# A two-layer encoder trunk on one core: first layer's memory keys projected ahead of the head pairs, one mask matmul a head, last group in two sums

## The chip, the cores and the metric

The kernel runs on one core of a Trainium2 chip. It is one program with five instruction streams: TensorE (PE), VectorE (DVE), ScalarE (ACT), GpSimd (POOL) and the queue of SyncE (SP), which loads the weights. The metric is the device time of one execution in microseconds (us).

## What is computed

Two layers work on x, 256 tokens by 2048 features in float32, with 256 memory tokens beside it. Each layer has a token mixer (layer 0: latent attention with 16 heads and a mask by chunks of 64 tokens; layer 1: stick-breaking attention with 16 heads, strictly causal), then 4 heads of attention into the memory, then a feed-forward network with a causal convolution of width 3. A root-mean-square norm stands before each.

```python
for i in range(DEPTH):                       # DEPTH = 2
    h = _rmsnorm(x, norm_mix[i])
    x = x + (_mla(h, cos, sin, ...) if i % 2 == 0 else _stick_breaking(h, ...))
    x = x + _mem_cross_attn(_rmsnorm(x, norm_mem_q[i]), _rmsnorm(mem, norm_mem_kv[i]),
                            mem_w_q[i], mem_w_kv[i], mem_w_o[i])
    x = x + _conv_ffn(_rmsnorm(x, norm_ffn[i]), ffn_w_in[i], ffn_conv_w[i], ffn_conv_b[i], ffn_w_out[i])
return _rmsnorm(x, norm_final)
```

In `_mla`, `down = h @ w_down` gives a query latent (512 wide, "cq"), a key/value latent ("ckv") and one rotary key ("krope"); each latent has a norm of its own. The keys of the memory are `hm @ w_kv[:, :512]` with `hm` the normed memory: they depend on nothing of x.

## The kernel before

**Weights.** All weights lie in HBM as one stream of 802 units of 128x1024 numbers (512 KB) in the order in which PE uses them (`stream_plan`). SP loads unit v into slot v mod 4 of `w_raw`. ACT copies it, rounded, to `w_hi` (`split`, L469), DVE writes the rest `w_raw - w_hi` to `w_lo` (L846). Both do this three units ahead of PE, in the same in-order queues as all their other work. Operands are split alike: ACT writes the high half (`operand_hi`, L487), DVE the low half (`operand_lo`, L868).

**Matmuls.** `unit` multiplies one weight unit. A chunk of 128 output features with one k takes high weights times [high|low] operand in one matmul 512 wide (L1309), plus low weights times high operand 256 wide (L1316): "two parts", whose sums lie in the two halves of a bank and are added later by `take_low` (ACT) and `take_sum` (DVE). With `parts=1` the first is done as two matmuls 256 wide (L1311, L1312) into the same half, and no adding is needed. Which phases use which is in `in_one_part`. A unit of two k has 4 chunks.

**Order in layer 0.** PE does cq (8 units), ckv (8), krope (2), then 8 stages of two heads each (`mla_stage`: rotary queries r, queries q, keys k, values v, one unit each, with the previous pair's attention between them), then memk0 (8 units, the memory keys, with the last pair's attention between them: `mla_tail`), then the output projection wo0 in four groups g, the memory attention and the feed-forward. Norm statistics: POOL squares and adds the tiles of a norm's input (`sum_squares`, L406, L408), PE averages the result over the partitions (`stat`, or `first_stat` for the first one, L1701, in ckv after its third unit), ACT takes the root and DVE refines it (`find_rstd`, L880 to L886). Then DVE scales the sums of a bank by it (`times_rstd`, L862).

**Memory.** POOL loads the memory in lots of four tiles into a ring of two lots (`load_mem`, L413). In `early_memory` ACT and DVE turn the first 8 tiles into operands during the stages of pairs 0 and 1, and the other 8 during memk0.

**Attention.** `mla_scores` gives one head's scores in bank 4: content and rotary products for the first 128 queries, a mask matmul in bf16 (64 columns, L1380), the same for the other 128, and a second mask matmul (L1383). DVE finds the row maxima (`row_tops`, L919), ACT takes the exponentials, DVE divides (`normalise`, L930), PE transposes (L1391) and multiplies by the values (L1400). `stick_logits` has two mask matmuls of 128 columns (L1492, L1494) in the same way.

**End.** The last group of the last feed-forward, out1_3 (22 units), is done in one part; then DVE adds its four tiles to x, the final norm follows, and the output is stored.

## Time and profile before

| | |
|---|---|
| median of 3 runs | 2391.85 us (2391.81 to 2393.09) |
| the profiled execution: time, span | 2391.88 us, 2389.7 us |
| mean granted clock of TensorE | 0.996 of full |
| PE, DVE, ACT, POOL busy | 99%, 70%, 52%, 13% of the span |
| weight loads | 802 of 512 KB, 3.3 us to landing; HBM 180 GB/s over the span |

The span runs from the first to the last instruction of the profiled execution. A matmul's end is modelled, so "busy" on PE covers a matmul's passage through the array and not only its columns; how fast PE goes is read from the starts of its matmuls.

### The profile page before, as it was taken

The numbers are of one execution on the slowest core, as the hardware profiler recorded it, in microseconds if no ns is written. First come the engines' busy times: TensorE is split into PE (matmuls) and PEld (weight loads), VectorE is DVE, ScalarE is ACT, GpSimd is POOL, SyncE is SP. The second block draws the span as 40 slices with busy tenths as digits, with TensorE's granted clock in tenths as the row PEclk, the third lists the DMA queues.
The fourth block names the chain that finished last, engine by engine and source line by source line (L and its number), as shares of the span: only waits on it lengthen the run. The fifth ranks groups of instructions, "written<-read, shape, count | busy, mean of one in ns | idle before, by whom it ended". The sixth has DMA issues, their size and how long they took to land.

```text
span 2389.7 us, 41908 instructions
## 1 busy us (share of the span) xinstructions
PE 2357.6 (99%) x14608; PEld 2107.5 (88%) x14608; DVE 1679.2 (70%) x2474; ACT 1234.0 (52%) x1860; POOL 300.7 (13%) x305
## 2 busy tenths in 40 slices
PE   9899999999999999999999999999999999999997
PEld 8799898888888888889899998889888888888897
DVE  8876678777877875555755556778778778775544
ACT  5445455655555654444555445455556556564442
POOL 7500225000000000111320000315000000001110
PEclk9999999999999999999999999999999999999999
DMA  7444554555555656555554445545555555556553
GB/s 260 145 137 162 187 176 156 193 189 184 192 187 183 194 191 204 190 189 185 177 177 164 163 164 170 191 160 174 188 184 192 189 180 195 192 180 197 187 187 122
DMA packets 122071, 432.42 MB, mean 181 GB/s; under 512 B 13424, under 2 KB 17776, under 8 KB 121968
## 3 DMA queue, kind: packets, MB, share of 16 engines
q1 hardware_dynamic: 118992, 423.94, 53.3%
q0 software_dynamic: 1440, 5.24, 0.7%
q10 hardware_dynamic: 1536, 1.80, 0.2%
q8 instruction: 72, 1.18, 0.2%
q14 instruction: 31, 0.25, 0.0%
HBM read 428.83 MB, written 2.10 MB: 180 GB/s over the span
## 4 chain that ended last, share of the span: by engine, by line
PE 93%; DVE 6%; ACT 1%; issue 0%; DMA 0%; DVEq 0%; SPq 0%; ACTq 0%
PE bank L1309 49%; PE bank L1316 28%; PE bank L1311 3%; PE bank L1312 3%; DVE w_lo L846 2%; PE bank L1331 2%; PE bank L1333 2%; PE bank L1332 2%; DVE h L868 1%; PE bank L1400 1%; ACT w_hi L469 0%; PE bank L1401 0%; PE bank L1391 0%; PE bank L1381 0%; DVE x L903 0%; PE bank L1491 0%
## 5 line engine op out<-in xcount | busy, mean ns | idle before, releaser
L846 DVE TENSOR_TENSOR w_lo<-w_raw,w_hi 128x1024 fp32r<-128x1024 f32 x802 | 1004.5, 1255 | 533.1 <-ACT w_hi L469 531.7
L469 ACT ACTIVATE w_hi<-w_raw 128x1024 fp32r<-128x1024 f32 x802 | 845.6, 1058 | 751.1 <-PE bank L1316 675.4
L1309 PE MATMUL bank<-h,w_hi 128*128 128x512 f32 x3392 | 1047.5, 396 | 3.2 <-DVE h L868 1.9
L1316 PEld LDWEIGHTS bank<-h,w_lo 128*128 128x128 f32 x3664 | 661.5, 188 | 138.8
L1316 PE MATMUL bank<-h,w_lo 128*128 128x256 f32 x3664 | 701.0, 279 | 0.0
L1309 PEld LDWEIGHTS bank<-h,w_hi 128*128 128x128 f32 x3392 | 525.9, 189 | 16.0 <-DVE h L868 2.1
L1309 PE MATMUL bank<-act,w_hi 128*128 128x512 f32 x1632 | 513.2, 396 | 0.0
L1316 PEld LDWEIGHTS bank<-act,w_lo 128*128 128x128 f32 x2272 | 403.9, 189 | 72.5
L1316 PE MATMUL bank<-act,w_lo 128*128 128x256 f32 x2272 | 443.5, 280 | 0.0
L1309 PEld LDWEIGHTS bank<-act,w_hi 128*128 128x128 f32 x1632 | 248.4, 189 | 0.1
L1311 PE MATMUL bank<-act,w_hi 128*128 128x256 f32 x640 | 168.9, 288 | 0.4 <-DVE attn L862 0.4
L1312 PE MATMUL bank<-act,w_hi 128*128 128x256 f32 x640 | 166.6, 284 | 0.0
L406 POOL TENSOR_TENSOR sq<-x 128x256 f32<-128x256 f32 x101 | 117.6, 1165 | 359.5 <-DVE x L903 354.6
L773 ACT ACTIVATE act<-tmp 128x256 f32 (+1 forms) x88 | 36.8, 418 | 180.7 <-DVE tmp L1224 180.7
L404 POOL TENSOR_TENSOR acc<-x 128x256 f32<-128x256 f32 x7 | 4.3, 614 | 994.1 <-DVE x L903 990.4
L763 ACT ACTIVATE tmp<-tmp,cols 128x256 f32<-128x256 f32 x176 | 104.5, 594 | 46.2 <-DVE tmp L862 46.1
L1311 PEld LDWEIGHTS bank<-act,w_hi 128*128 128x128 f32 x640 | 123.7, 193 | 2.3 <-issue 0.6
L1312 PEld LDWEIGHTS bank<-act,w_hi 128*128 128x128 f32 x640 | 123.7, 193 | 0.1
L408 POOL TENSOR_TENSOR acc<-acc,sq 128x256 f32<-128x256 f32 x126 | 118.6, 941 | 9.9
L851 DVE TENSOR_TENSOR tot<-low,bank 128x256 f32<-128x256 f32 x272 | 112.3, 413 | 0.1
L1215 DVE SCALAR_TENSOR_TENSOR tmp<-tmp,cols 128x256 f32<-128x256 f32 x176 | 85.3, 485 | 23.9 <-DVE tmp L1212 1.6
L476 ACT ACTIVATE low<-bank 128x256 f32<-128x256 f32 x272 | 97.9, 365 | 0.0
(153 smaller groups left out, 1943.7 us busy)
## 6 DMA issues: line engine op xcount, KB each, us to landing
w_raw<-stream SPq DMA_DIRECT2D x802, 512.0 KB, 3.3
tmp<-mem_in POOLq DMA_DIRECT2D x10, 512.0 KB, 4.8
out<-attn SPq DMA_DIRECT2D x5, 256.0 KB, 2.7
x<-x_in SPq DMA_DIRECT2D x4, 256.0 KB, 5.3
x<-x_in SPq DMA_DIRECT2D x2, 512.0 KB, 8.5
out<-attn ACTq DMA_DIRECT2D x3, 256.0 KB, 2.2
cols<-cols_in ACTq DMA_DIRECT2D x1, 420.5 KB, 5.1
mats<-mats_in ACTq DMA_DIRECT2D x1, 320.0 KB, 5.8
```

The source lines that it names most:

```text
L406: step(nc.gpsimd.tensor_tensor(sq[:, :], tile, tile, ALU.mult))
L408: step(nc.gpsimd.tensor_tensor(acc[:, :], acc[:, :], sq[:, :], ALU.add))
L469: nc.scalar.activation(w_hi[:, s, :], w_raw[:, s, :], ACT.Copy).then_inc(hi_split, 1)
L476: nc.scalar.activation(low[:, t % 2, :], banks[bank][:, TOK:2 * TOK], ACT.Copy).then_inc(low_copied, 1)
L763: nc.scalar.activation(conv[:, j % 2, :], u_ext[:, j % 2, 2:TOK + 2], ACT.Identity, scale=conv_col(2, 4 * g + j + is_up * FT, it), bias=co ...
L846: nc.vector.tensor_tensor(w_lo[:, s, :], w_raw[:, s, :], w_hi[:, s, :], ALU.subtract).then_inc(lo_split, 1)
L851: nc.vector.tensor_tensor(tot[:, t % 2, :], low[:, t % 2, :], banks[bank][:, 0:TOK], ALU.add).then_inc(tile_summed, 1)
L1215: nc.vector.scalar_tensor_tensor(conv[:, j % 2, :], u_ext[:, j % 2, 0:TOK], conv_col(0, c, it), conv[:, j % 2, :], ALU.mult, ALU.add).then ...
L1309: mm(bank[:, :], w_hi[:, s, c:c + P], a, start=first and i == 0, stop=False)
L1311: mm(bank[:, 0:TOK], w_hi[:, s, c:c + P], a[:, 0:TOK], start=first and i == 0, stop=False)
L1312: mm(bank[:, 0:TOK], w_hi[:, s, c:c + P], a[:, TOK:2 * TOK], start=False, stop=False)
L1316: ins = mm(bank[:, 0:TOK], w_lo[:, s, c:c + P], a[:, 0:TOK], start=False, stop=last and i == len(ks) - 1)
```

## The change

**Memory keys first.** memk0 moves in the weight stream and on every engine from behind the head pairs to between ckv and krope. Its 16 operand tiles are made by ACT and DVE during the last two units of cq, in ckv and in the first two units of memk0 (`KEYS_AT`), with semaphores of their own (`key_hi`, `key_lo`); POOL issues two loads of the memory after six tiles of its first sum of squares, the third after the thirteenth, behind a wait for four key tiles, and the fourth after the sixteenth. The memory is loaded again for its norm and again for the values' operands: 14 loads in all, where there were 10. The sums of memk0 are added unscaled into `mem_k` during krope and scaled in wo0_0. The steps that stood in krope (low halves of the ckv latent, table angles, roots) move to memk0. `early_memory` goes.

**Last heads beside wo0_0.** The last pair's attention (`mla_tail`) stands between the units of wo0_0, and so do the norm of the memory, the four scalings of `mem_k` and the operands of memory tiles 8 to 15 for the values. For this the banks of the groups are exchanged (`half`), in layer 1 too (`stick_banks`, `STICK_Z`).

**One mask matmul a head.** The mask operand is stored twice side by side, and one bf16 matmul (2x64 columns; stick-breaking 2x128) writes both places at the end of the scores.

**Last group in two sums.** out1_3 does its first 19 units in two parts into one set of banks, the last 3 in one part into another. ACT and DVE add the first sum to x beside the last 3 units.

```diff
-        (phase[:3] != "out" or phase[-2:] == "_3")
+        (phase[:3] != "out" or phase == "out0_3")
...
+def two_sums(phase):
+    return phase == "out1_3"
...
@@ -79,6 +88,7 @@
         if layer == 0:
             phase("cq", 8, 4, 4)
             phase("ckv", 8, 4, 4)
+            phase("memk0", 8, 4, 4)
             phase("krope", 2, 1, 1)
...
-        phase(f"memk{layer}", 8, 4, 4)
+        if layer:
+            phase(f"memk{layer}", 8, 4, 4)
...
+FIRST_SUM = {0: (0, 1), 1: (2,), 2: (3,)}
...
-            return 0 if g % 2 else 4
-        EARLY_MEMORY = {(0, 2): (0,), (0, 3): (1, 2), (1, 0): (3,), (1, 1): (4,), (1, 2): (5,), (1, 3): (6, 7)}
...
+            return 4 if g % 2 else 0
+        KEYS_AT = {("cq", 6): (0, 1), ("cq", 7): (2, 3), ("ckv", 0): (4, 5), ("ckv", 1): (6, 7), ("ckv", 3): (8,), ("ckv", 4): (9,),
+                   ("ckv", 5): (10,), ("ckv", 6): (11, 12), ("ckv", 7): (13,), ("memk0", 0): (14,), ("memk0", 1): (15,)}
...
             if layer == 0:
-                return (h[:, k, :], act[:, 8 + k, :], True) if first else (act[:, 8 + k, :], act[:, 8 + k, :], False)
-            return (act[:, HEADS + k, :], act[:, HEADS + k, :], False) if first else (h[:, k, :], act[:, k, :], True)
+                return act[:, k, :], act[:, 8 + k, :]
...
             for n in range(KT):
+                if n == 6:
+                    load_mem(0)
+                    load_mem(1)
+                if n == 13:
+                    pool.wait_ge(key_lo, 4)
+                    load_mem(2)
                 pool.wait_ge(x_landed[x_lot(n)], 16)
                 sum_squares("mix0", n, KT, x[:, n, :])
-            load_mem(0)
-            load_mem(1)
+            pool.wait_ge(key_lo, 8)
+            load_mem(3)
             for name in ("cq", "ckv"):
...
+            pool.wait_ge(key_lo, KT)
+            load_mem(0)
+            load_mem(1)
...
-                if l == 5:
+                first_keys("ckv", l)
+            for l in range(8):
+                split(PLAN["memk0"][0] + l + AHEAD)
+                if l < LT:
+                    times_rstd(latent[:, LT + l, :], whole("ckv", 7, l, 4 + l), rstd_x).then_inc(latent_ready, 1)
+                first_keys("memk0", l)
+                n = l - 1
+                if 0 <= n < LT:
+                    k = HEADS + LT + n
+                    operand_lo(act[:, k, TOK:2 * TOK], latent[:, LT + n, :], GAIN["ckv"] + n, act[:, k, 0:TOK], OP0["ckv"] + n)
+                if l == 2:
                     rope_angle()
-                if l == 7:
+                if l == 4:
                     rope_cos()
+                if l == 6:
+                    find_rstd("cq", rstd_q, 5, D_MODEL / LORA)
...
-                for n in (2 * l, 2 * l + 1):
-                    times_rstd(latent[:, LT + n, :], whole("ckv", 7, n, 4 + n), rstd_x).then_inc(latent_ready, 1)
-                for n in (2 * l, 2 * l + 1):
-                    k = HEADS + LT + n
-                    operand_lo(act[:, k, TOK:2 * TOK], latent[:, LT + n, :], GAIN["ckv"] + n, act[:, k, 0:TOK], OP0["ckv"] + n)
-                if l == 0:
-                    find_rstd("cq", rstd_q, 1, D_MODEL / LORA)
+                for j in (2 * l, 2 * l + 1):
+                    take_sum(PLAN["memk0"][2] + j, j, to=mem_k[:, j, :])
+            find_rstd("ckv", rstd_kv, 6, D_MODEL / LORA)
...
+                        if g == 0 and l in ahead_of:
+                            ahead_of[l]()
                         split(PLAN[f"wo{layer}_{g}"][0] + l + AHEAD)
                         if g == 0 and l == 0:
-                            find_rstd(f"memkv{layer}", rstd_m[:, :], half(0) + 3)
+                            find_rstd(f"memkv{layer}", rstd_m[:, :], MEMORY_STAT[layer])
                         if g == 0 and l < 4:
-                            times_rstd(mem_k[:, l, :], take_sum(PLAN[f"memk{layer}"][2] + l, l), rstd_m).then_inc(scaled, 1)
+                            keys = take_sum(PLAN[f"memk{layer}"][2] + l, half(1) + l) if layer else mem_k[:, l, :]
+                            times_rstd(mem_k[:, l, :], keys, rstd_m).then_inc(scaled, 1)
+                        if g == 0 and l in tail:
+                            tail[l]()
+                        if layer == 0 and g == 0 and l < 4:
+                            mem_lo(layer, 8 + 2 * l, True)
+                            mem_lo(layer, 9 + 2 * l, True)
...
+                        side(l)
+                        if two_sums(phase):
+                            for j in FIRST_SUM.get(l - (n - LAST_WHOLE), ()):
+                                first_sum = take_sum(t0 + j, half(g + 1) + j)
+                                nc.vector.tensor_tensor(x[:, 4 * g + j, :], x[:, 4 * g + j, :], first_sum, ALU.add).then_inc(first_added, 1)
             def no_side(l):
...
                 mm(b[:, 0:P], q_sb[:, e, i, 0:P], k_sb[:, e, i, 0:P], start=True, stop=False)
-                mm(b[:, 0:P], qr_sb[:, e, 0:P], kr_sb[:, i, 0:P], start=False, stop=False)
-                mm(b[:, CHUNK:P], MASK_ROWS, MASK_COLS, start=False, stop=True)
-                mm(b[:, P:3 * P], q_sb[:, e, i, P:2 * P], k_sb[:, e, i, :], start=True, stop=False)
-                mm(b[:, P:3 * P], qr_sb[:, e, P:2 * P], kr_sb[:, i, :], start=False, stop=False)
-                mm(b[:, 2 * P + CHUNK:3 * P], MASK_ROWS, MASK_COLS, start=False, stop=True).then_inc(s_done, 1)
+                mm(b[:, 0:P], qr_sb[:, e, 0:P], kr_sb[:, i, 0:P], start=False, stop=True)
+                mm(b[:, P:3 * P], q_sb[:, e, i, P:2 * P], k_sb[:, e, i, :], start=False, stop=True, skip_group_check=True)
+                mm(b[:, P:3 * P], qr_sb[:, e, P:2 * P], kr_sb[:, i, :], start=False, stop=True, skip_group_check=True)
+                late_keys = b.rearrange("p (t n) -> p t n", t=2)[:, :, CHUNK:P]
+                mm(late_keys, MASK_ROWS, MASK_COLS, start=False, stop=True, skip_group_check=True).then_inc(s_done, 1)
...
-                mm(z[:, 0:P], IDENT_BF, NEG_STRICT, start=False, stop=True, skip_group_check=True)
                 mm(z[:, TOK:TOK + P], k_sb[:, e, i, P:2 * P], q_sb[:, e, i, P:2 * P], start=False, stop=True, skip_group_check=True)
-                mm(z[:, TOK:TOK + P], IDENT_BF, NEG_STRICT, start=False, stop=True, skip_group_check=True).then_inc(z_done, 1)
+                diagonal = z.rearrange("p (t n) -> p t n", t=2)[:, :, 0:P]
+                mm(diagonal, IDENT_BF, NEG_STRICT, start=False, stop=True, skip_group_check=True).then_inc(z_done, 1)
...
+            def first_memory():
+                for l in range(8):
+                    pe.wait_ge(key_lo, 2 * l + 2)
+                    unit(PLAN["memk0"][0] + l, (2 * l, 2 * l + 1), 4 * P, lambda j: j, lambda k: kept_memory(0, k)[0], l == 0, l == 7,
+                         lambda j: pe.wait_ge(latent_ready, j + 1))
+                    if l == 5:
+                        pe.wait_ge(latent_ready, LT + 2)
+                        stat("cq", 5)
+                pe.wait_ge(latent_ready, LT + 3)
+                stat("ckv", 6)
...
+                        if g == layer:
+                            taken(j)
+                        elif g == 1 - layer:
                             if j == 0:
...
-                    group(f"wo{layer}_{g}", HEADS, half(g), from_act, free, heads_ready if g == 0 else None)
+                    def attend_last(l):
+                        if l in tail:
+                            tail[l]()
+                    group(f"wo{layer}_{g}", HEADS, half(g), from_act, free, heads_ready if g == 0 else None, attend_last if g == 0 else None)
...
-                          parts=1 if in_one_part(f"out{layer}_{g}") else 2)
+                    if two_sums(phase):
+                        v0, n = PLAN[phase][0], FT // 2
+                        m = n - LAST_WHOLE
+                        for l in range(m):
+                            unit(v0 + l, (2 * l, 2 * l + 1), 4 * P, lambda j: half(g + 1) + j, from_act, l == 0, l == m - 1, free_of(phase))
+                        for l in range(m, n):
+                            unit(v0 + l, (2 * l, 2 * l + 1), 4 * P, lambda j: half(g) + j, from_act, l == m, l == n - 1,
+                                 lambda j: summed(PLAN[f"out{layer}_{g - 1}"][2] + j), parts=1)
+                    else:
...
-            stat("cq", 1)
             for l in range(2):
-                unit(v0 + l, tuple(range(8 * l, 8 * l + 8)), P, lambda j: 2, from_h, l == 0, l == 1,
-                     lambda j: pe.wait_ge(latent_ready, 3), parts=1)
+                unit(v0 + l, tuple(range(8 * l, 8 * l + 8)), P, lambda j: 4, from_h, l == 0, l == 1,
...
-            summed(PLAN["out1_2"][2] + 3)
-            stat("final", half(3) + 3, [last_squares(n) for n in range(KT - 4, KT)])
+            pe.wait_ge(first_added, 4)
```

ACT's queue changes as DVE's does: it makes each high half just ahead of the low half shown here. `krope` goes to bank 4, `r0` to bank 7.

Three places, as the instruction streams have them. First POOL, from the thirteenth tile of the first sum of squares to its end and the loads behind it. Before:

```order
L406 TENSOR_TENSOR sq<-x 128x256
L408 TENSOR_TENSOR acc<-acc,sq 128x256
L406 TENSOR_TENSOR sq<-x 128x256
L408 TENSOR_TENSOR acc<-acc,sq 128x256
L406 TENSOR_TENSOR sq<-x 128x256
L408 TENSOR_TENSOR acc<-acc,sq 128x256
L406 TENSOR_TENSOR sq<-x 128x256
L408 TENSOR_TENSOR acc<-acc,sq 128x256
L406 TENSOR_TENSOR sq<-x 128x256
L410 TENSOR_TENSOR acc<-acc,sq 128x256
L413 DMA tmp<-mem_in 128x4x256 x2
```

Now:

```order
L437 TENSOR_TENSOR sq<-x 128x256
L439 TENSOR_TENSOR acc<-acc,sq 128x256
L444 DMA tmp<-mem_in 128x4x256
L437 TENSOR_TENSOR sq<-x 128x256
L439 TENSOR_TENSOR acc<-acc,sq 128x256
L437 TENSOR_TENSOR sq<-x 128x256
L439 TENSOR_TENSOR acc<-acc,sq 128x256
L437 TENSOR_TENSOR sq<-x 128x256
L441 TENSOR_TENSOR acc<-acc,sq 128x256
L444 DMA tmp<-mem_in 128x4x256
L435 TENSOR_TENSOR acc<-attn_49 128x256
```

The load that stands between the thirteenth and the fourteenth tile waits until DVE has made four key tiles; it and the two loads after the sixth tile were behind the sum.

Then PE, from the last chunk of ckv (bank7) on. Before:

```order
L1312 MATMUL bank7<-h,w_hi 128x256
L1316 MATMUL bank7<-h,w_lo 128x256 x2
L1346 MATMUL bank1<-acc,mats 128x256
L1311 MATMUL bank2<-h,w_hi 128x256
L1312 MATMUL bank2<-h,w_hi 128x256
```

Now:

```order
L1394 MATMUL bank7<-h,w_hi 128x256
L1398 MATMUL bank7<-h,w_lo 128x256 x2
L1391 MATMUL bank0<-act,w_hi 128x512 x2
L1398 MATMUL bank0<-act,w_lo 128x256 x2
L1391 MATMUL bank1<-act,w_hi 128x512 x2
L1398 MATMUL bank1<-act,w_lo 128x256 x2
L1391 MATMUL bank2<-act,w_hi 128x512 x2
```

The statistic of cq (bank1) and krope (bank2) followed ckv at once; now the 8 units of memk0 follow, with that statistic after the sixth.

Last DVE, at the start of the unit stretch that holds the last pair's attention: memk0 before, wo0_0 now (small: row maxima and their reciprocals; act<-tmp: operands of the memory). Before:

```order
L846 TENSOR_TENSOR w_lo<-w_raw,w_hi 128x1024
L868 SCALAR_TENSOR_TENSOR act<-tmp,cols,act 128x256 x2
L846 TENSOR_TENSOR w_lo<-w_raw,w_hi 128x1024
L919 TENSOR_REDUCE small<-bank4 128x1 x2
L922 TENSOR_SCALAR small<-small 128x2
L868 SCALAR_TENSOR_TENSOR act<-tmp,cols,act 128x256 x2
L927 RECIPROCAL small<-small 128x2
L930 TENSOR_SCALAR attn_49<-attn_49,small 128x128
L930 TENSOR_SCALAR attn_49<-attn_49,small 128x256
```

Now:

```order
L902 TENSOR_TENSOR w_lo<-w_raw,w_hi 128x1024
L942 TENSOR_SCALAR attn_49<-bank7 128x258
L944 SCALAR_TENSOR_TENSOR attn_49<-rstd_m 128x258
L946 TENSOR_TENSOR attn_49<-attn_49 128x258
L948 SCALAR_TENSOR_TENSOR rstd_m<-attn_49,rstd_m 128x258
L919 TENSOR_TENSOR attn_49<-attn_49,rstd_m 128x256
L925 SCALAR_TENSOR_TENSOR act<-tmp,cols,act 128x256 x2
L902 TENSOR_TENSOR w_lo<-w_raw,w_hi 128x1024
L919 TENSOR_TENSOR attn_49<-attn_49,rstd_m 128x256
L984 TENSOR_REDUCE small<-bank4 128x1 x2
L987 TENSOR_SCALAR small<-small 128x2
L925 SCALAR_TENSOR_TENSOR act<-tmp,cols,act 128x256 x2
L992 RECIPROCAL small<-small 128x2
L995 TENSOR_SCALAR attn_49<-attn_49,small 128x128
L995 TENSOR_SCALAR attn_49<-attn_49,small 128x256
```

Ahead of the division of head 14's probabilities (the last row or two) there now stand five more instructions of the norm's root and scaling (L942 to L919) and one more scaling.

## Rows read from the trace of the kernel before

**Rows 1.** the page, part 1: engine, busy time, share of the span, instructions
```profile
PE 2357.6 (99%) x14608; PEld 2107.5 (88%) x14608; DVE 1679.2 (70%) x2474; ACT 1234.0 (52%) x1860; POOL 300.7 (13%) x305
```

**Rows 2.** waits of PE, 56 to 120 us: total us, times, longest
```profile
PE bank L1411 <- DVE attn L862: 4.4, 2, 3.6
PE bank L1391 <- DVE attn L930: 2.4, 3, 1.4
PE bank L1331 <- DVE attn L862: 1.6, 1, 1.6
PE bank L1346 <- POOL acc L410: 1.1, 1, 1.1
PE bank L1311 <- DVE attn L862: 0.4, 1, 0.4
```

**Rows 3.** PE alone in four stretches: length, busy (count), granted clock, DMA share, GB/s
```profile
72.60:79.30 6.70, 5.65 (x24) 0.50 0.49 157
82.90:86.10 3.20, 2.77 (x13) 0.50 0.54 164
2280.00:2300.00 20.00, 20.00 (x116) 1.00 0.55 187
2340.00:2360.00 20.00, 20.00 (x169) 1.00 0.48 160
```

**Rows 4.** PE by time at the layer change: start, length, what
```profile
1145.98 0.50 PE L1309 MATMUL bank<-h,w_hi 128*128 128x512 f32 x1 [1.88 <-DVE h L868]
```

**Rows 5.** POOL by time: its squares of the input tiles, then two loads
```profile
18.11 1.48 POOL L406 TENSOR_TENSOR sq<-x 128x256 f32<-128x256 f32 x1
...
31.10 1.48 POOL L406 TENSOR_TENSOR sq<-x 128x256 f32<-128x256 f32 x1
...
38.27 1.60 POOL L410 TENSOR_TENSOR acc<-acc,sq 128x256 f32<-128x256 f32 x1
39.81 1.67 POOL L413 DMA_DIRECT2D tmp<-mem_in  x2
```

**Rows 6.** PE by time: the first sum over squares
```profile
42.10 0.38 PE L1701 MATMUL bank<-acc,mats 128*128 128x256 f32 x1
```

**Rows 7.** DVE by time: operands and splits, beside POOL and without it
```profile
28.72 1.71 DVE L868 SCALAR_TENSOR_TENSOR h<-x,cols,h 128x256 fp32r<-128x256 f32 x2
30.36 6.54 DVE L846 TENSOR_TENSOR w_lo<-w_raw,w_hi 128x1024 fp32r<-128x1024 f32 x4
...
52.58 0.70 DVE L960 CAST attn<-attn 128x256 f32<-128x256 int32 x1
...
56.17 0.29 DVE L967 TENSOR_SCALAR attn<-attn 128x256 f32<-128x256 f32 x1
...
207.05 0.88 DVE L868 SCALAR_TENSOR_TENSOR act<-tmp,cols,act 128x256 fp32r<-128x256 f32 x2 [1.38 <-ACT act L487]
```

**Rows 8.** DVE by time: last pair's probabilities, later a norm
```profile
203.71 1.23 DVE L846 TENSOR_TENSOR w_lo<-w_raw,w_hi 128x1024 fp32r<-128x1024 f32 x1 [0.48 <-ACT w_hi L469]
...
208.04 0.55 DVE L930 TENSOR_SCALAR attn<-attn,small 128x128 f32<-128x128 f32 x2
...
229.41 0.42 DVE L880 TENSOR_SCALAR attn<-bank 128x258 f32<-128x258 f32 x1
...
231.70 0.43 DVE L886 SCALAR_TENSOR_TENSOR rstd_m<-attn,rstd_m 128x258 f32<-128x258 f32 x1
```

**Rows 9.** PE by time: transposes of head 14
```profile
209.47 0.38 PE L1391 MATMUL bank<-mats,attn 128*128 128x128 f32 x2
```

**Rows 10.** PE by time: a head's scores and its first mask
```profile
202.80 0.19 PE L1380 MATMUL bank<-masks 128*128 128x64 bf16 x1
202.83 0.68 PE L1381 MATMUL bank<-attn 128*128 128x256 f32 x2
203.34 0.59 PE L1382 MATMUL bank<-attn 128*128 128x256 f32 x2
```

**Rows 11.** the page, part 6: loads of the memory, KB, us to landing
```profile
tmp<-mem_in POOLq DMA_DIRECT2D x10, 512.0 KB, 4.8
```

More of the change, by code:

```diff
@@ L710, in projections @@
                 v0 = PLAN[f"memq{layer}"][0]
-                again = [k for k in range(KT) if kept_memory(layer, k)[2]]
+                again = AGAIN[layer]
                 side = residual_side(f"wo{layer}_3", norm, 3, half(3), EARLY)
@@ L805, in ffn @@
                 for g in range(1, 4):
-                    stage(f"out{layer}_{g}", FT // 2, residual_side(f"out{layer}_{g - 1}", last_norm, g - 1, half(g), EARLY))
+                    phase, side = f"out{layer}_{g}", residual_side(f"out{layer}_{g - 1}", last_norm, g - 1, half(g), EARLY)
+                    n, (v0, _, t0) = FT // 2, PLAN[phase]
+                    for l in range(n):
+                        split(v0 + l + AHEAD)
+                        side(l)
+                        if two_sums(phase):
+                            for j in FIRST_SUM.get(l - (n - LAST_WHOLE), ()):
+                                take_low(t0 + j, half(g + 1) + j, chunk_of(phase, n - LAST_WHOLE - 1, j))
             def no_side(l):
@@ L1156, in projections @@
                 side = residual_side(f"wo{layer}_3", norm, 3, half(3), EARLY)
-                again = [k for k in range(KT) if kept_memory(layer, k)[2]]
+                again = AGAIN[layer]
                 for l in range(8):
@@ L1257, in ffn @@
                 for g in range(1, 4):
-                    stage(f"out{layer}_{g}", FT // 2, residual_side(f"out{layer}_{g - 1}", last_norm, g - 1, half(g), EARLY))
+                    phase, side = f"out{layer}_{g}", residual_side(f"out{layer}_{g - 1}", last_norm, g - 1, half(g), EARLY)
+                    n, (v0, _, t0) = FT // 2, PLAN[phase]
+                    for l in range(n):
+                        split(v0 + l + AHEAD)
+                        side(l)
+                        if two_sums(phase):
+                            for j in FIRST_SUM.get(l - (n - LAST_WHOLE), ()):
+                                first_sum = take_sum(t0 + j, half(g + 1) + j)
+                                nc.vector.tensor_tensor(x[:, 4 * g + j, :], x[:, 4 * g + j, :], first_sum, ALU.add).then_inc(first_added, 1)
             def no_side(l):
```

226 lines of the change are left out of this document (127 added, 99 removed).

## Prediction

> **What bounds the kernel now.** I read the page first. PE is busy 99% of the span [rows 1], so only two things can pay: time that PE loses, and matmuls that take less. The page's slices show the granted clock nowhere below nine tenths, but a slice is 60 us long; so next I read who PE waited for, and the granted clock, in short stretches. The waits are in one place: between 56 and 120 us PE waits nine times, 9.9 us in all [rows 2]. The longest, 3.6 us at L1411, is the rotation of the shared key behind DVE's work on the latents; the others are DVE's too, but for one (POOL, 1.1). In the same place the clock stood at half, 0.50, in two stretches of 6.70 and 3.20 us, with PE busy 5.65 and 2.77 us of them [rows 3]: that is the lower of TensorE's levels, 1.2 GHz, and the reader should note what preceded it, the wait of 3.6 us. At the layer change PE idles 1.88 us [rows 4] and no half clock follows. Elsewhere PE runs without a wait, and there its own rate decides: in 20 us it starts 116 matmuls of a two-part phase (four to a chunk) or 169 of a one-part phase (six to a chunk) [rows 3], so a chunk takes 4 x 20/116 = 0.690 or 6 x 20/169 = 0.710 us, and a unit of four chunks 2.76 or 2.84 us. A few records may be missing, so the difference is good to some 0.007.
>
> **The sum.** It goes from the profiled execution, 2391.88 us (span 2389.7 and 2.2 around it), which is the median of the runs, 2391.85, to 0.03. About 0.2%, 4.8 us, is what a measurement of this kernel can tell from no change.
>
> *Memory keys first.* The 8 units are moved and cost PE the same. What they can give back is what PE loses at 56 to 120 us: 9.9 us of waits; half of 5.65 + 2.77 us of busy time at half clock, 4.2; and, an estimate, 0.15 for each of nine waits, 1.4, since a matmul is shown for 0.38 us [rows 6] though starts come 0.118 apart, so that a wait is counted late. Together 15.5 us. The eight units are 22 us of PE work that waits for nothing of the latents, put in front of everything that does; so the waits of 3.6, 1.1 and 0.4 us go, and the half clock with them. The wait before the first values (L1331, 1.6) has a chain of its own, rotation, a split, scaling, and only the norm of ckv (2.7 us) leaves it: I keep half, 0.8. Of the remaining 3.2 (the second at L1411, three at L1391), pairs 1 and 2, I keep 1.2: the early memory operands, 0.44 us each, go from DVE, but POOL's squares of the memory stay beside it.
>
> Something new is late: POOL. Its first sum of squares ended at 39.87 and PE took it at 42.10 without a wait [rows 5, 6], 2.2 us of room. Now two loads after the sixth tile take 1.67 us [rows 5], so the thirteenth tile is done at 32.8 instead of 31.1, and there POOL waits for the fourth key tile. DVE's queue gives that: from 30.36 the splits of units 8 and 9, two keys, the split of unit 10, two keys. A split is 1.63 us beside POOL (6.54 for four) and 1.23 without, an operand 0.86 or 0.44 [rows 7, 8], successive ones overlap by 0.07, and POOL is idle from 32.8: about 36.1. Then a load, 0.8, and three tiles. Six tiles took 12.99 us from 18.11 to 31.10, 2.17 each, beside one split and two operands a unit, which is the mixture that DVE has again: 43.4. PE waits 1.3 us (bounds: 0, and 3.6 at the 2.9 us a tile of the last three, 31.10 to 39.87). Nothing waits for the later loads: keys 8 to 11 are wanted ten us after theirs. So 1.3 + 0.15 + 0.8 + 1.2 = 3.5 us stay: **-12.0** (bounds -15.5 and -5).
>
> Here the Trainium skill's page "SBUF — State Buffer" (Who interferes with whom) has a rule against the change: a DVE instruction with two SBUF inputs and a GpSimd instruction that reads SBUF lock each other out for a whole instruction. By that rule the trace agrees (1.63 against 1.23, 0.86 against 0.44); what more of it would do is the second rival.
>
> *Last heads beside wo0_0.* The attention is as it was; new ahead of `normalise` of head 14 on DVE are the memory norm's root, 229.41 to 232.13, 2.7 us [rows 8], and two scalings of 0.4. Before, DVE had a wait of 0.48 there [rows 8], the division ended at 208.59 and PE transposed at 209.47 [rows 8, 9], 0.88 later. The statistic's matmuls, now ahead of wo0_0, give about 0.8 more (two passes of 0.38 [rows 6] as an estimate). So 2.7 + 0.8 - 0.5 - 0.9 - 0.8: **+1.3** (bounds 0 and 3.5). Queued behind it are splits, three units ahead of PE: covered. Head 15 has no norm ahead of it.
>
> *Masks.* The first mask starts at 202.80, 0.03 before the next matmul, whose two passes are shown for 0.68 us, where the two of the next one, just as wide, are shown for 0.59 [rows 10]. So a mask costs 0.03 + 0.09, some 0.11 us, most of it the passage to bf16 and back. One of two goes: 16 heads, 1.8 us; I take 1.6, for in a pair DVE's chain is nearly as long as PE's. In layer 1 the same, but the new mask has 128 more columns than an old one, 0.06 at 0.118 for 256: 0.8 to 1.8, I take 1.2. **-2.8** (bounds 0 and -3.6).
>
> *Last group.* 19 units x 4 chunks x 0.020: **-1.5** (bounds -1.0 and -2.0). The four takes and additions, under 4 us of DVE and ACT, lie beside the last three units, 8.5 us, in which no split is left. What follows the last matmul is as it was. The exchange of banks costs nothing: the waits on them name the same events.
>
> Sum: -12.0 + 1.3 - 2.8 - 1.5 = -15.0; 2391.88 - 15.0 = **2376.9 us**.
>
> The Trainium skill's page "TensorE: Matmul & The Clock Gate" (Back-to-back issue gap) prices a lone matmul stream at N/2.4 + 2.5 ns, with a floor for small N. By it a two-part chunk would be 650 ns and a one-part chunk 655, the last group 0.4 us instead of 1.5, and a doubled mask as dear as two; the sum would be 2380.8. Rows 3 and 10 say otherwise, 20 ns a chunk and 0.11 a mask.
>
> **Rivals.** *DVE becomes the bound.* From 30.36 to the split of the seventh memory unit DVE has 15 splits, 16 keys, 6 other low halves, 7 scalings (0.42), a root (2.7) and the table angle, 52.58 to 56.46, 3.9 us [rows 7]: with overlaps taken off 34.4 us free of POOL, 49.5 all beside it. PE wants that split at 42.1 + 1.3 + 0.25 + 5 x 2.84 + 6 x 2.76 + 0.4 = 74.8. POOL works in some 40% of the stretch, so DVE is there at 30.4 + 40.4 + 2 of waiting = 72.8. With POOL beside it all the time it would be 5 to 7 us late. The price taken is half of that, 3.5: 2380.4 us. For it: DVE is hardly idle from 5 to 40 us. Against: the room of 2 us.
>
> *The sum comes late and the clock falls.* Three tiles at 2.9 us make PE wait 3.6: 2.3 more, and a gap as long as the one before the half clock [rows 2], which halves the next 6.7 us, 3.3: 2382.5 us.
>
> *A mask saves only its own columns*, the passage staying in whatever place, and the 20 ns being missing records: masks and last group nothing, -10.7: 2381.2 us. The rule of the page on TensorE above leads to the same for the masks, and nearly for the group. Rows 10 speak against it: the dear part stands right behind the mask and goes with it [rows 10].
>
> *Slower: the memory tiles land late.* Keys 0 to 3 stand in ACT's and DVE's queues ahead of the split of unit 10, which PE wants at 39.3. From landing to that split pass two keys and two splits, 4.5 us, so every us after 34.8 is one lost. The loads are issued by 18.2 and such a load takes 4.8 [rows 11]: room of 11 us. To eat the 15.0 they must land at 50, or at 46.5 with the clock falling; landing at 52, the kernel takes 2394 us. That the weights are loaded in the same us is all that speaks for it.
>
> **How the numbers follow.** The forecast 62%, DVE the bound 15%, late sum 10%, own columns only 6%; two or three of these together, within 0.2%, 4%; late tiles 3%. So faster 0.93, same 0.04, slower 0.03. The range, 2371.5 to 2383.0, has at its low end nearly all bounds of gain (15.5 + 3.6 + 2.0, with 0.7 for wo0_0) and takes in the first three rivals.
>
> **What the profile will show.** If right: between 56 and 130 us waits of PE of 2 to 3.5 us in all and clock 1.00; a wait of 1 to 2 us at the first statistic near 42; a wait of 1 to 2 us at the transposes of head 14 in wo0_0; 16 + 16 mask matmuls and chunks 0.1 us earlier for each; 19 units of out1_3 at 2.76. Wrong would be: a wait for w_lo at the seventh or eighth memory unit (DVE), half clock after 43 (POOL), ACT waiting for the tmp load at 28 (tiles), or the same starts behind a mask (columns).

## Result and profile after

The changed kernel takes **2386.0 us** (median of 15 runs, 2383.76 to 2390.59), the kernel before 2392.15 beside it (15 runs, 2390.26 to 2394.92): ratio 0.9977, 95% interval 0.9970 to 0.9984. So it is faster, clear of the noise, but by some 6 us (a quarter of a per cent) where 15 were forecast; the time lies 3 us above the range. The profiled execution took 2386.63 us, its span is 2384.8, 4.9 less than before.

The page first. PE's busy time answers to [rows 1]: 5.0 us less, as much as the span, and its share is still 99%. So the page doesn't tell what went wrong.

```profile
PE 2352.6 (99%) x14424; PEld 2097.3 (88%) x14424; DVE 1687.6 (71%) x2490; ACT 1237.1 (52%) x1872; POOL 303.5 (13%) x309
```

PE's waits from 40 to 140 us of the changed kernel, which answer to [rows 2] (total us, times, longest):

```profile
PE bank L1493 <- DVE attn L919: 3.0, 2, 2.3
PE bank L1428 <- POOL acc L441: 2.8, 1, 2.8
PE bank L1803 <- POOL acc L441: 1.7, 1, 1.7
PE bank L1413 <- DVE attn L919: 1.2, 1, 1.2
PE bank L1473 <- DVE attn L995: 0.7, 1, 0.7
```

That is 9.4 us, where before had 9.9 and the forecast left 3.3. Two rows are waits for POOL: the first statistic (L1803), forecast, and the statistic of the key latents (L1428), not forecast and now the longest single wait. The rotations (L1493) wait 3.0 where they waited 4.4, the first values (L1413) 1.2 where they waited 1.6.

PE alone, by stretches (length, busy, count, granted clock, DMA share, GB/s), beside the first two of [rows 3]:

```profile
83.12:89.95 6.83, 5.94 (x26) 0.50 0.76 223
89.95:107.02 17.07, 12.93 (x100) 1.00 0.46 160
107.02:110.43 3.41, 3.41 (x18) 0.50 0.60 186
110.43:140.00 29.57, 28.71 (x219) 1.00 0.46 156
```

The half clock is back too: 5.94 + 3.41 us of busy time at 0.50, 4.7 us lost, where before lost 4.2. They moved 10.5 and 24 us later (from 72.6 and 82.9), and neither went away.

How the 4.9 us between the two spans are made up, by the starts on PE. The masks and the last group are sized by the traces of the experiments below, and the first line is what remains:

| part | forecast | measured |
|---|---|---|
| memory keys first | -12.0 | -0.9 |
| last heads beside wo0_0 | +1.3 | +1.3 |
| masks | -2.8 | -3.0 |
| last group in two sums | -1.5 | -1.8 |
| up to the first statistic | 0 | -0.5 |

The +1.3 is the start of head 14's transposes, 1.39 us after the matmul before it, where matmuls there follow each other in 0.12. The first statistic could have started at 41.56, 0.54 earlier than before [rows 6]. Most of that is PE's wait for the low half of the first weights, 0.75 us at 7.48 where the kernel before waited 1.32 at 7.89. It is scatter and not the change: PE's program is the same up to there in both kernels and in the experiments below, and in the two of them in which PE didn't wait for POOL this statistic started at 41.45 and at 42.82.

**What the statistic waited for.** POOL by time in the changed kernel: squares of the query latents' last tile, then those of the key latents.

```profile
56.59 1.60 POOL L441 TENSOR_TENSOR acc<-acc,sq 128x256 f32<-128x256 f32 x1
75.77 1.56 POOL L435 TENSOR_TENSOR acc<-attn 128x256 f32<-128x256 f32 x1 [17.58 <-PE bank L1428]
...
82.28 1.58 POOL L441 TENSOR_TENSOR acc<-acc,sq 128x256 f32<-128x256 f32 x1
```

And PE by time in the same place:

```profile
75.03 0.60 PE L1428 MATMUL bank<-acc,mats 128*128 128x256 f32 x2
...
84.01 1.19 PE L1428 MATMUL bank<-acc,mats 128*128 128x256 f32 x2 [2.81 <-POOL acc L441]
84.99 0.85 PE L1434 MATMUL bank<-mats,acc 128*128 128x1 f32 x4
```

POOL has one accumulator, `acc`. It was done with the query latents at 58.19 and could start on the key latents only when PE's statistic had read `acc`, at 75.3, since the changed program puts that statistic behind the sixth memory unit. This is the first hand-over. POOL sat idle for 17.58 us, then needed 8.1, and PE had two units, 5.6 us, to put beside them.

**What the rotations waited for.** The two rotations on PE, then DVE by time behind that statistic, and ACT's split ahead of DVE's:

```profile
98.50 0.70 PE L1493 MATMUL bank<-attn,mats 128*128 128x256 f32 x2 [0.62 <-DVE attn L919]
...
104.40 0.70 PE L1493 MATMUL bank<-attn,mats 128*128 128x256 f32 x2 [2.33 <-DVE attn L919]
```

```profile
84.87 0.86 DVE L908 TENSOR_TENSOR attn<-low,bank 128x256 f32<-128x256 f32 x2
91.95 1.32 DVE L902 TENSOR_TENSOR w_lo<-w_raw,w_hi 128x1024 fp32r<-128x1024 f32 x1 [6.21 <-ACT w_hi L510]
93.19 0.86 DVE L908 TENSOR_TENSOR attn<-low,bank 128x256 f32<-128x256 f32 x2
94.08 0.43 DVE L942 TENSOR_SCALAR attn<-bank 128x258 f32<-128x258 f32 x1
```
```profile
90.78 1.06 ACT L510 ACTIVATE w_hi<-w_raw 128x1024 fp32r<-128x1024 f32 x1 [7.89 <-PE bank L1398]
```

The statistic was there at 85.8. DVE sat idle for 6.2 us of what followed and began the root (L942) 8.2 us later. In its queue the root stands behind a split, the one for the fourth unit after the first of the shared key; that split waits for ACT's, and ACT's for a weight buffer which PE frees with that first unit. This is the second hand-over. Then root, scaling, rotation, scaling follow each other, and PE waits for each.

### The profile page after: what moved, and what is told of

Read it like the earlier page. It is cut to its first block, busy times and chain, and to the rows that moved or that the text cites. A ratio compares the mean times of both kernels' runs of the same rounds, so it can differ in the third digit from the quotient of the medians.

```text
span 2384.8 us, 41584 instructions
## 1 busy us (share of the span) xinstructions
PE 2352.6 (99%) x14424; PEld 2097.3 (88%) x14424; DVE 1687.6 (71%) x2490; ACT 1237.1 (52%) x1872; POOL 303.5 (13%) x309
## 4 chain that ended last, share of the span: by engine, by line
PE 93%; DVE 5%; ACT 1%; POOL 1%; DMA 1%; issue 0%; DVEq 0%; SPq 0%; ACTq 0%; POOLq 0%
PE bank L1391 50%; PE bank L1398 28%; PE bank L1393 3%; PE bank L1394 3%; PE bank L1413 2%; PE bank L1415 2%; PE bank L1414 2%; DVE w_lo L902 2%; DVE h L925 1%; PE bank L1482 1%; ACT w_hi L510 1%; DMA w_raw<-stream 1%; PE bank L1483 0%; PE bank L1473 0%; DVE x L968 0%
## 5 line engine op out<-in xcount | busy, mean ns | idle before, releaser
L1391 PE MATMUL bank<-act,w_hi 128*128 128x512 f32 x1816 | 571.2, 396 | 0.0
L1398 PEld LDWEIGHTS bank<-act,w_lo 128*128 128x128 f32 x2304 | 414.3, 189 | 80.6
L1398 PE MATMUL bank<-act,w_lo 128*128 128x256 f32 x2304 | 448.5, 279 | 0.0
L1391 PEld LDWEIGHTS bank<-act,w_hi 128*128 128x128 f32 x1816 | 276.5, 189 | 0.3
L1393 PE MATMUL bank<-act,w_hi 128*128 128x256 f32 x488 | 127.9, 287 | 0.0
L1394 PE MATMUL bank<-act,w_hi 128*128 128x256 f32 x488 | 125.7, 283 | 0.0
L1393 PEld LDWEIGHTS bank<-act,w_hi 128*128 128x128 f32 x488 | 93.4, 191 | 1.7
L1394 PEld LDWEIGHTS bank<-act,w_hi 128*128 128x128 f32 x488 | 93.5, 192 | 0.1
```

What stands on the lines that cost most here:

```text
L1391: mm(bank[:, :], w_hi[:, s, c:c + P], a, start=first and i == 0, stop=False)
L1393: mm(bank[:, 0:TOK], w_hi[:, s, c:c + P], a[:, 0:TOK], start=first and i == 0, stop=False)
L1394: mm(bank[:, 0:TOK], w_hi[:, s, c:c + P], a[:, TOK:2 * TOK], start=False, stop=False)
L1398: ins = mm(bank[:, 0:TOK], w_lo[:, s, c:c + P], a[:, 0:TOK], start=False, stop=last and i == len(ks) - 1)
```

## Experiments

All times are medians; each ratio is to the kernel before on the same chip, with its 95% interval. The diffs are against the changed kernel where nothing else is said.

### The statistic of the query latents two units earlier

```diff
-                    if l == 5:
+                    if l == 3:
                         pe.wait_ge(latent_ready, LT + 2)
                         stat("cq", 5)
```

> The changed kernel, with PE's statistic of the query latents behind the fourth memory unit instead of the sixth. Theory A (one accumulator): POOL may start on the key latents' squares only when that statistic has read its accumulator; in the changed kernel it started at 75.8 us, idle for 17.6 us before, and its 8.1 us of work ended 2.8 us after PE had run out of units at 81. The statistic is moved two units, 5.5 us, ahead; so POOL starts near 70.2, ends near 78.5, the wait of 2.8 us at the second statistic is gone, and the half clock that began at 83 with it (6.8 us, 3.4 lost): 5 to 6.5 us less than the changed kernel, ratio to before 0.9951 to 0.9958. Theory B (POOL's own pace, or the last latent tile of DVE, sets the end): POOL starts earlier but ends past 81; less than 1 us is gained. Theory C (the half clock comes from the many waits of the stretch): the wait goes, but a half clock of 6 to 7 us stays somewhere between 80 and 110; about 3 us gained, ratio 0.9964.

2381.94 us, 0.9959 (0.9945 to 0.9972). POOL by time, then PE by time:

```profile
70.10 1.56 POOL L435 TENSOR_TENSOR acc<-attn 128x256 f32<-128x256 f32 x1 [12.02 <-PE bank L1428]
...
76.62 0.74 POOL L441 TENSOR_TENSOR acc<-acc,sq 128x256 f32<-128x256 f32 x1
```
```profile
80.93 0.60 PE L1428 MATMUL bank<-acc,mats 128*128 128x256 f32 x2
```

POOL starts 5.7 us earlier, PE takes the sum without a wait, and the clock stays at 1.00 until 101: theory A for the accumulator, B falls. Of C something is left: a half clock of 3.42 us stands at 101.1, behind the two waits at the rotations, which grew to 3.5 us together. 4.1 us are gained, where A expected 5 to 6.5.

### The root ahead of the split that stood in its way

```diff
             for l in range(2):
                 split(PLAN["krope"][0] + l + AHEAD)
                 for j in (2 * l, 2 * l + 1):
                     take_sum(PLAN["memk0"][2] + j, j, to=mem_k[:, j, :])
-            find_rstd("ckv", rstd_kv, 6, D_MODEL / LORA)
+                if l == 0:
+                    find_rstd("ckv", rstd_kv, 6, D_MODEL / LORA)
```

and the same for `root` on ACT.

> The changed kernel, with the root of the key latents' norm on DVE and ACT between the two units of the shared key, ahead of the split that stands in front of it, instead of behind both. Theory A (a root queued behind a split): DVE idled 6.2 us ahead of that split, with the statistic already there at 85.8, and began the root at 94.1; now it begins near 86 and the rotations no longer wait: the waits of 0.6, 2.3 and most of 1.2 us at the two rotations and the first values go, and the second half clock of 3.4 us (1.7 lost) with them: 4 to 5.5 us less than the changed kernel, ratio 0.9954 to 0.9961. Theory B (DVE's own work on rotation and scaling sets these times): the waits only move, under 1.5 us gained, ratio 0.9971 or more. The wait of 2.8 us at the statistic stays in both.

2381.76 us, 0.9955 (0.9942 to 0.9969): 4.2 less than the changed kernel. The root begins at 86.42 instead of 94.08, and PE waits at neither rotation; the 2.8 us at the statistic stay. Theory A, but for the first values, which were to lose most of their wait and still wait 1.4.

### Both

> Both of the two edits before in one kernel. Theory A for both: no wait of PE over 1.3 us between 45 and 120 us and no half clock there; 9 to 12 us less than the changed kernel, about 2376, ratio 0.9930 to 0.9940: the forecast's own account of the memory keys. If the losses of that stretch are set by DVE's total work instead, 3 to 5 us less than the changed kernel, ratio 0.9955 to 0.9965, and half clock somewhere past 80.

2381.97 us, 0.9953 (0.9939 to 0.9967). **Two edits that win 4 us each win 4 us together**: that is the rival's number, and a half clock of 6.83 us stands behind 98.7. The wait at the statistic is gone; a wait at the second rotation is back (PE by time):

```profile
97.87 0.70 PE L1495 MATMUL bank<-attn,mats 128*128 128x256 f32 x2 [2.12 <-DVE attn L920]
99.76 0.55 PE L1415 MATMUL bank<-w_hi,act 128*128 128x256 f32 x1 [1.19 <-DVE attn L920]
```

DVE by time, in the same kernel, ahead of it:

```profile
82.30 3.07 DVE L903 TENSOR_TENSOR w_lo<-w_raw,w_hi 128x1024 fp32r<-128x1024 f32 x2
...
88.02 0.72 DVE L947 TENSOR_TENSOR attn<-attn 128x258 f32<-128x258 f32 x1
88.78 0.85 DVE L949 SCALAR_TENSOR_TENSOR attn<-attn 128x258 f32<-128x258 f32 x1
```

DVE is no longer idle there; it is slow. With the statistic earlier, POOL goes on to its squares of the memory from 82.1 us, and so works beside DVE in just the stretch in which each DVE operation is waited for.

Part of it is the clock. Two of the five runs took 2379.7 and 2379.9 us at a mean clock of 0.998, the other three 2382.0 to 2382.8 at 0.996; the profile is of one of the three, and it also has a half clock of 3.4 us at the layer change, where the changed kernel's has none.

### POOL's squares of the memory held back

With both edits:

```diff
             load_mem(1)
+            pool.wait_ge(v_stored, 1)
             mem_norm(0)
```

> The kernel with both edits (statistic and root early), and POOL's squares of the memory held back until the first pair's values are stored. There PE still waited 2.3 us at the second rotation and 1.4 at the first values, behind a DVE that never idled from 74 to 103 us but for its roots. Theory A (POOL beside it makes DVE slow: its splits took 1.5 us from 82 to 99 instead of 1.23, operations of 0.42 took 0.7 to 0.96): without POOL DVE wins 2.5 to 3 us from 82 to 99; the two waits fall from 3.6 us to 1.0 to 1.5, and the half clock of 6.8 us behind them to none or 3.4: 2.5 to 5 us less than with both edits alone (2382.0), ratio to before 0.9935 to 0.9945. Theory B (the chain rotation, scaling, rotation has 2.7 us of its own and the work of one short unit, 1.4 us, over it): the wait at the second rotation stays over 1.2 us; under 1.5 us gained, ratio 0.9948 or more.

2378.3 us, 0.9934 (0.9921 to 0.9948): 3.7 less than with both edits alone, theory A. The same two splits and the same root, DVE by time:

```profile
82.39 2.36 DVE L904 TENSOR_TENSOR w_lo<-w_raw,w_hi 128x1024 fp32r<-128x1024 f32 x2
...
87.40 0.43 DVE L948 TENSOR_TENSOR attn<-attn 128x258 f32<-128x258 f32 x1
87.86 0.43 DVE L950 SCALAR_TENSOR_TENSOR attn<-attn 128x258 f32<-128x258 f32 x1
```

Neither rotation waits, and no half clock is left before the layer change. The work of DVE from 82.3 to 97.5 us (length, busy, count), with POOL beside it and then without:

```profile
82.30:97.50 15.20, 13.94 (x19) 1.00 0.75 248
```
```profile
82.30:97.50 15.20, 13.91 (x25) 1.00 0.72 241
```

The same 13.9 us of busy time hold 19 instructions beside POOL and 25 without it; of the same chain, the scaling ahead of the second rotation (L920, here L921) starts at 97.39 beside POOL and at 94.65 without it, 2.7 us earlier. This is the rule that the forecast cited from the Trainium skill's page "SBUF — State Buffer" (Who interferes with whom); the trace agrees: operations with both inputs in SBUF are longer beside POOL (0.72 and 0.85 against 0.43 in the root), while the additions with one input in a bank (L909, here L910) take 0.86 and 0.87 us for two. It costs time here because PE waits for a chain of such operations.

Of the 3.7 us between the two spans (2380.4 and 2376.7) PE's waits from 40 to 140 us give 0.8 (5.2 and 4.4) and the half clock behind them 2.9 (half of 5.79 us of busy time). Both profiles have the half clock at the layer change. So most of what POOL cost here was paid at the clock, and the last section shows that this price isn't the same in every execution.

The same edit on the changed kernel alone, where the statistic is late:

> The changed kernel with only POOL's squares of the memory held back until the first pair's values are stored. POOL worked beside DVE from 91.6 us on. Theory A (that slows DVE's root, rotations and splits between 94 and 106 us by 2.5 to 3 us in sum): the waits of 0.6 and 2.3 us at the rotations shrink to under 0.5 together, the wait of 2.8 at the second statistic stays with its half clock; 2.5 to 4.5 us less than the changed kernel. Theory B (DVE's late start on the root alone decides, at 94.1): waits of 2 us or more stay at the second rotation; under 1 us gained.

2382.77 us, 0.9963 (0.9949 to 0.9976), 2.6 less than the changed kernel on that chip (2385.35). The rotations wait 0.3 us in all instead of 3.0; the 2.8 at the statistic stay, and PE's waits from 40 to 140 us fall from 9.4 to 7.7 in all. Theory A again: the wait at the rotations goes with the late root or with POOL, whichever of the two is taken away.

### The third load of memory tiles behind the first sum

```diff
-                if n == 13:
-                    pool.wait_ge(key_lo, 4)
-                    load_mem(2)
                 pool.wait_ge(x_landed[x_lot(n)], 16)
                 sum_squares("mix0", n, KT, x[:, n, :])
+            pool.wait_ge(key_lo, 4)
+            load_mem(2)
             pool.wait_ge(key_lo, 8)
             load_mem(3)
```

> The changed kernel, with POOL's load of the third four memory tiles behind the sixteenth square of the first sum instead of ahead of the fourteenth. Theory A: POOL idled 3.2 us there for the fourth memory key, and the first statistic on PE waited 1.7 us because of it; now POOL ends its sum near 40, PE takes it at 41.4 without a wait: 1.7 to 1.9 us less than the changed kernel, ratio 0.9970, and the later load still lands before its first key is wanted. Rival: the third load now lands late, and ACT waits for it ahead of a split (a key wanted near 50): PE waits for a split near 60 and the gain is gone. A second rival: the sum comes no earlier, as POOL beside more of DVE's operands runs at 2.9 us a tile: under 0.5 gained.

2383.22 us, 0.9964 (0.9950 to 0.9978). POOL by time; in the changed kernel that load stood at 36.89, with 3.16 us idle before it:

```profile
38.52 1.60 POOL L441 TENSOR_TENSOR acc<-acc,sq 128x256 f32<-128x256 f32 x1
40.07 0.79 POOL L444 DMA_DIRECT2D tmp<-mem_in  x1
43.03 0.75 POOL L444 DMA_DIRECT2D tmp<-mem_in  x1 [2.17 <-DVE act L924]
```

The first statistic no longer waits, and no split comes late: theory A. By the medians 2.8 us are won, where 1.7 to 1.9 were expected; the wait at the second statistic is 2.0 here and not 2.8, since POOL's squares of the key latents took 7.2 us (73.73 to 80.97) and not 8.1.

### One mask a head, on the kernel before

The edit is the change's own, in `mla_scores` and `stick_logits`, and nothing else of the change.

> The kernel before with one mask matmul a head in place of two, in both layers, and nothing else changed. By the forecast: 1.6 us less in layer 0 and 1.2 in layer 1, 2.8 in all (ratio 0.9988). By the rival (a mask saves only its own columns): 0 to 0.5. Read from the changed kernel's trace, which had gained 2.0 us over layer 1's mixer: 1.5 + 2.0 = 3.5 (ratio 0.9985).

2389.97 us, 0.9987 (0.9978 to 0.9996): 2.5 less. The trace splits it. In layer 1 the masks' first and last start are 277.5 us apart before and 275.5 here (instructions of the mask line; before, then this kernel):

```profile
L1494 PE MATMUL bank<-masks x16: 219/219/219, 1176.1 to 1453.6; 128*128 128x128 bf16 x16
```
```profile
L1495 PE MATMUL bank<-masks x16: 272/272/273, 1176.0 to 1451.5; 128*128 128x256 bf16 x16
```

So 2.0 us, where 1.2 were forecast. In layer 0 the masks of head 4 and of head 12 start 62.11 us apart before and 61.64 here: 0.06 a head, some 1.0 in all, where 1.6 were forecast. By the starts the scores of every head are 0.11 shorter, as the forecast read it from [rows 10], but in every second head the next interval is longer by as much (10.36 us from mask to mask in both kernels). The rival that a mask saves only its own columns (0 to 0.5 us) falls.

### The last group in one sum again

```diff
-    return phase == "out1_3"
+    return False
```

with the phase in one part again and the last statistic's bank and wait as before.

> The changed kernel, with the last group of the last output projection in one part and one sum again, as before; all else stays. By the forecast it takes 1.5 us more than the changed kernel (1.0 to 2.0): its units are 2.84 us instead of 2.76. If the additions in the last three units had cost something at the end: 0 to 1 us. Ratio to before 0.9983 where the changed kernel has 0.9977; the profile's last 70 us decide.

2387.09 us, 0.9975 (0.9964 to 0.9986), beside 2386.0 and 0.9977: by the medians alone this can't be told from nothing. The trace can. PE from behind its last wait for the residual in layer 1 to the final statistic, the changed kernel and then this one:

```profile
1634.48 0.73 PE L1391 MATMUL bank<-h,w_hi 128*128 128x512 f32 x2 [0.65 <-DVE x L968]
...
2370.15 1.03 PE L1431 MATMUL bank<-low,mats 128*128 128x256 f32 x4
```
```profile
1636.20 0.73 PE L1391 MATMUL bank<-h,w_hi 128*128 128x512 f32 x2 [0.65 <-DVE x L968]
...
2373.66 1.03 PE L1431 MATMUL bank<-low,mats 128*128 128x256 f32 x4
```

735.67 against 737.46: 1.8 us, of 1.5 forecast (1.0 to 2.0).

### The wait in wo0_0

First the division ahead of the operands:

```diff
+                        if g == 0 and l + 1 in ahead_of:
+                            ahead_of[l + 1]()
                         if layer == 0 and g == 0 and l < 4:
                             mem_lo(layer, 8 + 2 * l, True)
```

and its old call removed.

> The changed kernel, with the division of head 14 on DVE ahead of the two memory operands that wait for ACT, and the same for head 15. The forecast put its 1.3 us in wo0_0 down to the root of the memory norm ahead of the division; in the trace that root ended at 225.2, 2.6 us before the head's scores, and DVE then idled 1.4 us for operands queued behind ACT's exponentials. Theory A (the operands): the wait of 1.1 us at the transposes of head 14 is gone or under 0.2; 1.0 to 1.3 us less than the changed kernel. Theory B (the root): the wait stays above 0.8.

2384.97 us, 0.9972 (0.9961 to 0.9982). Then the root behind both divisions (`find_rstd` of the memory at the sixth unit, its scalings at the seventh and eighth):

> The changed kernel, with the root of the memory norm and the four scalings of its keys moved behind both heads' divisions in wo0_0 (fifth to seventh unit), the memory operands left where they are. Theory A (the operands are the cause): the wait at the transposes of head 14 stays at 0.8 to 1.2 us, no gain. Theory B (the root, as the forecast had it): it is gone, 1.0 to 1.3 us less.

2386.2 us, 0.9978 (0.9969 to 0.9987). The changed kernel itself ran beside the two:

> The changed kernel itself, unaltered, on the chip of the three kernels beside it, to compare them with it and not only with before: median near 2386.0, single runs from 2383.8 to 2390.6 as before, the long ones with the lower mean clock (0.994 against 0.998), ratio 0.9977.

2385.35 us (9 runs, 2383.41 to 2388.53), 0.9973 (0.9963 to 0.9982). In time neither edit can be told from it. By the waits of PE from 200 to 260 us, the changed kernel has one, the kernel with the division first none, and the one with the root behind another one in its place, with a half clock of 3.4 us behind it in its profile; the first row is the changed kernel's, the second that of the root behind:

```profile
PE bank L1473 <- DVE attn L995: 1.1, 1, 1.1
```
```profile
PE bank L1484 <- DVE act L1000: 1.9, 1, 1.9
```

So the forecast's cause stands, and the operands are a second one: take either away and the wait at head 14 goes. The expectation ahead of these two runs misread a row: 227.87 is when DVE took head 14's row maxima, 3 us after its scores were done (224.9), because of the root and what followed it. Moving the root only hands the wait on: its 2.7 us then stand ahead of head 14's low half, for which PE waits before it weighs head 15's values.

### All of it

Statistic early, root early, third load behind the first sum, POOL held back, division first:

> All in one: statistic early, root early, third memory load behind the first sum, POOL's memory squares held back, and in the unit of wo0_0 in which head 14's probabilities are divided the division ahead of the memory operands on DVE instead of behind them (and so for head 15). Theory: the waits of the changed kernel at the first statistic (1.7), at the second statistic (2.8), at the first rotation (0.6) and in wo0_0 (1.1) are gone, of the 3.5 us at the second rotation and the first values 1 to 2 stay, and of 5.1 us lost at half clock at most 1.7: 11 to 13 us less than the changed kernel's 2386: 2373 to 2375, ratio 0.9920 to 0.9928. If DVE's own work is the bound of the whole stretch to 105 us, what is won at 41 and 83 comes back as a wait there: 2377 to 2380.

**2375.16 us** (2374.84 to 2376.28), 0.9925 (0.9912 to 0.9939): 17 us less than before, 11 less than the changed kernel. 2373 to 2375 was expected, with a ratio of 0.9920 to 0.9928: the time is 0.2 above, the ratio inside. Waits of PE from 40 to 240 us are down to 2.8:

```profile
PE bank L1475 <- DVE attn L996: 1.6, 4, 0.6
PE bank L1415 <- DVE attn L920: 1.2, 1, 1.2
```

and the granted clock stays at 1.00 until past the last matmul of the last group.

## Why the prediction was wrong

**The step that failed** is in *Memory keys first*: "The eight units are 22 us of PE work that waits for nothing of the latents, put in front of everything that does; so the waits of 3.6, 1.1 and 0.4 us go, and the half clock with them." The units are 22 us of cover, but for what stands behind them only if the engines under the cover may use it. They may not, in two places. POOL's squares of the key latents are bound to PE's statistic of the query latents through one accumulator, and the change puts that statistic behind the sixth unit: of 22 us of cover POOL got 5.6 for work of 8.1. The wait of 1.1 became one of 2.8. DVE's root of the key latents stands behind a split that PE's progress releases: at the two rotations 3.0 of 4.4 us stayed (3.6 and 0.8 before, 0.6 and 2.3 now). The forecast went through POOL's queue only to the first statistic and said "Nothing waits for the later loads"; for the latents it counted work against cover, without following who hands what to whom. The two experiments that take one hand-over away each win 4 us, and with both taken away and POOL off DVE's chain the kernel takes 2378.3, where the forecast came to 2376.9: the amount to be had was about right, and the change doesn't take it. That all five edits give 2375.2 is no closer hit, since the load moved and the division first remove two waits, of 1.3 us each, that the forecast had kept.

**The price of waits at the clock** follows from that. The half clock was to go with the waits (4.2 us); the waits stayed, and 4.7 us are lost to it. The forecast also counted nine waits where [rows 2] have eight, which makes its term for late counting 0.15 us too large and changes nothing.

**First statistic.** Right: PE waits 1.7 us, forecast 1.3. POOL waited for the fourth key tile to 36.89 (forecast 36.1), and its sum was done at 43.26 (43.4).

**Rivals.** *DVE becomes the bound* named the right trait at the wrong place: no split of a memory unit was late, but on the chain of the rotations POOL beside DVE costs 3.7 us, the clock included, once the other two causes are gone. *The sum comes late and the clock falls*: the wait came, 1.7 and not 3.6, and at 44 us the clock stood at 1.00. *Own columns only* and *tiles land late* didn't happen: the load took 5.3 us, and no split waited for it.

**wo0_0.** Right in size (1.3) and in cause, with a second cause beside it that the forecast didn't name, the memory operands in ACT's queue behind the exponentials.

**Masks and last group.** Right: -3.0 and -1.8 for -2.8 and -1.5. That the masks' sum came out is partly luck, two misses that cancel: 1.0 for 1.6 in layer 0 and 2.0 for 1.2 in layer 1. In layer 1 a mask costs 0.13 us and not 0.08, over the bound of 1.8; in layer 0 every second head gives its 0.11 back. The rule of the Trainium skill's page "TensorE: Matmul & The Clock Gate" (Back-to-back issue gap), by which both would have been worth 0.4 together, is not borne out: a chunk in four matmuls is 0.024 us shorter than in six (1.8 over 76 chunks), not 0.005.

## What to carry to other kernels

Work put in front of a wait covers it only if each engine under it can start: follow the buffers of which there is only one (an accumulator, a bank) and each queue's order from hand-over to hand-over, not the sums of work against cover. A root or a scaling on a dependent chain belongs ahead of a split for a unit far ahead, since that split may itself wait for PE. And when a chain of short DVE operations is what PE waits for, keep POOL's work on SBUF out of just that stretch.

## What the runs showed of the hardware

**The same wait doesn't always cost clock.** The kernel with the division first has, up to wo0_0, the program of the changed kernel and the same wait of 2.81 us at the second statistic; yet PE's clock, at 84 to 90 us there, stood at 1.00 (first row), where the changed kernel's was 0.50. The other way round, behind the same 1.9 us at the layer change the kernel with POOL held back was at 0.50 (second row) and the changed kernel at 1.00:

```profile
84.00:90.00 6.00, 6.00 (x49) 1.00 0.85 296
```
```profile
1135.30:1138.60 3.30, 3.30 (x10) 0.50 0.51 197
```

All fourteen profiles of this case have this wait of 1.9 us, and five of them a half clock of 3.4 us behind it.

The scatter goes with the clock: over the 24 runs of the changed kernel the mean granted clock goes from 0.998 (2383.80 and 2383.41 us) down to 0.994 (2390.59 and 2388.53). So waits of 1.9 to 2.8 us were followed by a half clock in some executions and not in others, at 1.7 us for a busy stretch of 3.4; a forecast of this kernel should hold it as a spread. What decides it in one execution stays open. The version with all edits, which has no wait over 1.2 us from 40 to 240 us, scatters by 1.4 us in its 5 runs, the changed kernel by 6.8 in its 15; five runs are few for a spread.
